# A two-layer hybrid trunk on one core: both attentions in blocks of two heads, and the turns of the experts' inner rows moved

## The reference

```
z = modulate(rms_norm(x)) @ w_in             # one projection feeds four mixers
A: p = softmax(q1 k1 / sqrt 32) - lam * softmax(q2 k2 / sqrt 32)
   ya = rms_norm(p @ v) * (1 - lam_init)     # 4 heads, 64 value columns a head
B: yb = hyena(z)                             # long convolution
C: window attention with sinks, 4 heads of 64, norm and rotation on q and k
D: yd = conformer convolution
acc = sum over the four of sigmoid(z @ w_gate + b) * (y @ w_branch)
x = x + g1 * (acc @ w_out)
experts: top 2 of 16; u = silu(x @ w1[e]) * (x @ w3[e]); y = u @ w2[e]
x = x + g2 * (weighted sum of the two experts' rows)
```

## Time and profile before

| | |
|---|---|
| median of the runs | 1540.88 us |
| profiled execution, its own time | 1544.08 us |
| its span | 1542.1 us |
| TensorE busy | 1445.8 us, 94% |
| VectorE, ScalarE, GpSimd busy | 757.9, 277.6, 165.9 us |
| TensorE, experts of both layers, waits for ScalarE's copy L1958 | 10.0 us in 14 |
| TensorE, experts of layer 1, waits for VectorE's L2731 | 7.2 us in 8 |
| HBM rate in the slices of layer 1's experts | 379, 418, 412, 422, 420, 238 GB/s |

### The profile page before, as it was taken

How to read it: one execution, slowest core, us unless ns; L and a number is a source line. 1 busy time by engine, 2 the same in 40 slices (tenths; PEclk the granted TensorE clock), 3 DMA queues, 4 the chain that set the end, 5 groups by cost and what they waited for, 6 DMA issues and landing times. The chain is left out here.

```text
span 1542.1 us, 17006 instructions
## 1 busy us (share of the span) xinstructions
PE 1445.8 (94%) x6200; PEld 718.8 (47%) x6200; DVE 757.9 (49%) x1689; ACT 277.6 (18%) x570; POOL 165.9 (11%) x156
## 2 busy tenths in 40 slices
PE   6999999789999999999999999899989999999987
PEld 2544644344444444632323233765777875433332
DVE  4297866646555879532122223686676635211112
ACT  3201101422232210411011011110242203000000
POOL 0000011001011210021111101001001210111000
PEclk9999999989999999999999999999999999999999
DMA  9420234101223453689999986425333695999996
GB/s 380 186 98 27 74 145 164 55 28 55 82 82 141 164 191 109 275 322 420 423 425 422 418 360 237 162 85 225 127 110 137 220 374 211 379 418 412 422 420 238
DMA packets 49536, 355.55 MB, mean 231 GB/s; under 512 B 6288, under 2 KB 6672, under 8 KB 22704
## 3 DMA queue, kind: packets, MB, share of 16 engines
q1 hardware_dynamic: 41360, 330.79, 54.3%
q0 software_dynamic: 4800, 14.24, 2.5%
q10 hardware_dynamic: 3296, 9.44, 1.6%
HBM read 343.88 MB, written 10.56 MB: 230 GB/s over the span
## 5 line engine op out<-in xcount | busy, mean ns | idle before, releaser
L1209 PE MATMUL ps<-hT,ring 128*128 128x512 f32 (+1 forms) x1344 | 452.6, 492 | 1.9 <-DVE hT L2334 1.3
L1209 PEld LDWEIGHTS ps<-hT,ring 128*128 128x128 f32 x1344 | 253.8, 192 | 177.0 <-issue 157.9
L1515 PE MATMUL ps<-ring,m 128*64 128x512 f32 x624 | 277.1, 595 | 12.7 <-ACT m L1958 8.0
L1515 PEld LDWEIGHTS ps<-ring,m 128*64 128x64 f32 x624 | 81.9, 137 | 185.4 <-issue 172.7
L2296 DVE SCALAR_TENSOR_TENSOR spare<-ring,crow 128x1024 bf16<-128x1024 f32 x120 | 155.8, 1298 | 4.1
L1222 PE MATMUL ps<-ring,hT 128*128 128x512 f32 (+1 forms) x352 | 125.1, 515 | 0.0
L2021 POOL TENSOR_TENSOR wide<-wide,gates 128x512 f32<-128x512 f32 (+1 forms) x48 | 69.6, 1450 | 395.9 <-DVE gates L2473 395.9
L1517 PE MATMUL ps<-n_,m 128*64 128x512 f32 x224 | 100.0, 595 | 0.0
L1310 PE MATMUL ps<-yT,ring 128*128 128x512 f32 (+1 forms) x256 | 94.5, 492 | 2.3 <-ACT n_ L1857 2.3
L1517 PE MATMUL ps<-wide,m 128*64 128x512 f32 x208 | 93.7, 597 | 0.0
L1222 PEld LDWEIGHTS ps<-ring,hT 128*128 128x128 f32 x352 | 66.7, 190 | 55.1 <-issue 51.4
(11 more groups left out here) (389 smaller groups left out, 1699.3 us busy)
## 6 DMA issues: line engine op xcount, KB each, us to landing
ring<-w SPq DMA_DIRECT2D x39, 2048.0 KB, 11.1
ring<-win SPq DMA_DIRECT2D x52, 1024.0 KB, 4.9
ring<-wmod SPq DMA_DIRECT2D x48, 1024.0 KB, 5.0
n_<-w SPq DMA_DIRECT2D x13, 2048.0 KB
hT<-w SPq DMA_DIRECT2D x13, 2048.0 KB, 16.6
wide<-w SPq DMA_DIRECT2D x13, 2048.0 KB
ring<-wbr SPq DMA_DIRECT2D x8, 1024.0 KB, 4.8
ring<-wout SPq DMA_DIRECT2D x4, 2048.0 KB, 11.9
```

Of the source, the lines that this page charges most:

```text
L1209: last = pe.matmul(b[:, 0:W], w[:, k, jj * P:(jj + 1) * P], hT[:, k, 0:W], start=(k == 0), stop=(k == KD - 1))
L1515: pe.matmul(ps[0:HALF, bnk, :], left[:, k, 0:HALF], even[k], start=(k == 0), stop=(k == n_k - 1), skip_group_check=True)
```

## The change

The lists of both attentions are written anew. `attention` now takes the products as pairs of a gate and a branch product and gives each block of two units its share of them (`share`): scores of both units; the value steps of a tile that ended in the block before; maxima and exponentials of both, then probabilities of both; the first group of the share (a gate product); in A the means of the ended tile; the next one or two groups; the transposes of both units; the rest of the share; the ended tile's `yR`; the block's share of the passes. In layer 0's A there are nine pairs of products for eight blocks, in layer 1's nine for four; in C eight for eight and for four. The last gate product of B, in C the first of C's own branch, stands ahead of the last tile's values; C's transposes come between A's last values and their means. `settled` goes.

In the experts, `turn_u` stands in the middle of the side's up products in layer 0. In layer 1 the mixing of pair e - 1 moves behind the up products of pair e, with `turn_u` between its two tiles; pair 0 turns as before. ScalarE's, VectorE's and SyncE's programs of the experts are unchanged.

```diff
--- before.py
+++ after.py
@@ -196,22 +196,6 @@
     return [s for g in spread(main, side) for s in g]
 
 
-def settled(groups):
...
-
 def mod_steps(l, chunks):
     out = []
     for c in chunks:
@@ -380,41 +364,54 @@
             return groups + turns
         return groups[:2] + [g for t in range(TILES - 2) for g in (groups[t + 2], turns[t])] + turns[-2:]
 
-    def attention(b):
+    def share(items, parts, n):
+
+        return items[-(-n * len(items) // parts):-(-(n + 1) * len(items) // parts)]
+
+    def attention(b, products, passes, behind):
+
         units = [(t, h) for t in range(tt) for h in HEADS_OF[b]]
-        groups, turn = [], []
-        for i in range(len(units) + 2):
-            group = []
-            if i < len(units) and i % 2 == 0:
-                group += [("T", ("s" + b, l, t, h, n)) for t, h in units[i:i + 2] for n in range(2 if b == "A" else 1)]
-            if i < len(units):
-                group += [("V", ("mx" + b, l, *units[i])), ("S", ("ex" + b, l, *units[i]))]
-            if 1 <= i <= len(units):
-                group += [("V", ("p" + b, l, *units[i - 1]))]
-            groups += [group] if group else []
-            if i >= 2:
-                t, h = units[i - 2]
-                groups += [g for g in turn[:1] if g]
-                turn = turn[1:]
-                groups += [[("T", ("pT" + b, l, t, h)), ("S", ("pTout" + b, l, t, h))]]
-                if h == 3 and b == "C":
-                    groups += [[("T", ("yC", l, t)), ("S", ("yToutC", l, t))]]
-                elif h == 3:
-                    groups += [[("T", ("yA", l, t)), ("S", ("ysqA", l, t))]]
-                    turn = [[("T", ("yM", l, t)), ("V", ("yrA", l, t))], [], [("T", ("yR", l, t)), ("V", ("ynA", l, t))]]
-        return groups + [g for g in turn if g]
+        values = lambda t: [("T", ("y" + b, l, t)), ("S", ("ysqA" if b == "A" else "yToutC", l, t))]
+        out, ended = [], []
+        pairs = [units[i:i + 2] for i in range(0, len(units), 2)]
+        for n, two in enumerate(pairs):
+            out += [("T", ("s" + b, l, t, h, q)) for t, h in two for q in range(2 if b == "A" else 1)]
+            normed = ended if b == "A" else []
+            out += [s for t in ended for s in values(t)]
+            for unit in two:
+                out += [("V", ("mx" + b, l, *unit)), ("S", ("ex" + b, l, *unit))]
+            out += [("V", ("p" + b, l, *unit)) for unit in two]
+            mine = share(products, len(pairs), n)
+            ahead = 3 if b == "A" and l else 2
+            steps = [g for pair in mine for g in pair]
+            out += steps[0]
+            out += [s for t in normed for s in (("T", ("yM", l, t)), ("V", ("yrA", l, t)))]
+            out += [s for g in steps[1:ahead] for s in g]
+            for t, h in two:
+                out += [("T", ("pT" + b, l, t, h)), ("S", ("pTout" + b, l, t, h))]
+            out += [s for g in steps[ahead:] for s in g]
+            out += [s for t in normed for s in (("T", ("yR", l, t)), ("V", ("ynA", l, t)))]
+            out += [s for g in share(passes, len(pairs), n) for s in g]
+            t, h = two[1]
+            ended = [t] if h == 3 else []
+        out += behind[0] + values(tt - 1)
+        if b == "A":
+            out += turns + [("T", ("yM", l, tt - 1)), ("V", ("yrA", l, tt - 1))]
+            out += behind[1] + [("T", ("yR", l, tt - 1)), ("V", ("ynA", l, tt - 1))]
+        return out
 
     o += merge(conformer[:12], spread(prepared("A") + projections, turned(with_conformer)))
-    units = attention("A")
-    half = len(units) // 2
-    turns = [g for g in prepared("C") if g[0][0] == "T"]
+    turns = [s for g in prepared("C") if g[0][0] == "T" for s in g]
     ropes = [[("V", ("rsC", l))]] + [g for g in prepared("C") if g[0][0] == "V"]
-    o += settled(spread(conformer[12:] + gate_groups(1, False),
-                        units[:half] + spread(units[half:], ropes) + turns))
-    o += settled(spread(spread(gate_groups(0, False), turned(in_c)), attention("C")))
+    two_of = lambda groups: [groups[i:i + 2] for i in range(0, len(groups), 2)]
+    products = two_of(conformer[12:] + gate_groups(1, False))
+    early_passes = [[]] * (len(ropes) - 2) if l == 0 else []
+    o += attention("A", products[:-1], early_passes + ropes, products[-1])
+    last_gates = gate_groups(2, False)
+    o += attention("C", two_of(gate_groups(0, False)), turned(in_c), last_gates[:1])
     net, spectrum = filter_groups(l + 1) if l + 1 < DEPTH else ([], [])
 
-    last_gates = gate_groups(2, False)
+    last_gates = last_gates[1:]
     n = len(last_gates) if l == 0 else len(last_gates) // 2
     o += merge(spread(last_gates[:n], turned(behind)) + last_gates[n:], net)
     o += gate_steps(l, (4, 5))
@@ -1518,9 +1515,9 @@
                                              start=(k == 0), stop=(k == n_k - 1), skip_group_check=True)
                         return last
 
-                    def four_quarters(bnk, left, quarters):
-
-                        for k in range(4):
+                    def four_quarters(bnk, left, quarters, ks=range(4)):
+
+                        for k in ks:
                             for g, (weights, k0, rows_, cols_) in enumerate(quarters):
                                 last = pe.matmul(ps[SIDE * g:SIDE * (g + 1), bnk, :], left[:, k0 + k, rows_:rows_ + SIDE],
                                                  weights[:, k0 + k, cols_], start=(k == 0), stop=(k == 3),
@@ -1531,8 +1528,8 @@
                         whole = slice(0, FE)
                         return [(even, 0, 0, whole), (odd, 0, SIDE, whole), (even, 4, 0, whole), (odd, 4, SIDE, whole)]
 
-                    def mix_block(first, last_, signal=True):
-                        for t in range(live(l)):
+                    def mix_block(first, last_, signal=True, tiles=range(live(l))):
+                        for t in tiles:
                             for half in range(2):
                                 last = pe.matmul(ps[:, 4 + 2 * t + half, :], mixing[:, t, :],
                                                  ysb[:, half * 512:(half + 1) * 512], start=first, stop=last_,
@@ -1541,14 +1538,17 @@
                                     last.then_inc(half_mixed, 1)
                         return last
 
-                    def mix(e):
+                    def mix(e, turn=None):
 
                         if not e:
                             pe.wait_ge(pieces_ready, l + 1)
                         pe.wait_ge(mixing_ready, e + 1)
                         pe.wait_ge(y_low, base + e + 1)
                         pe.wait_ge(y_high, base + e + 1)
-                        mix_block(e == 0, e == PAIRS - 1).then_inc(y_mixed, 1)
+                        mix_block(e == 0, e == PAIRS - 1, True, range(0, 1))
+                        if turn is not None:
+                            turn_u(turn)
+                        mix_block(e == 0, e == PAIRS - 1, True, range(1, 2)).then_inc(y_mixed, 1)
 
                     def gate_and_up(e):
 
@@ -1568,8 +1568,6 @@
                             if behind_first(l, e):
                                 pe.wait_ge(side_y_ready, e)
                             four_quarters(7, side_xT, split_k(wg, wg2)).then_inc(side_gate_done, 1)
-                        if not side and e:
-                            mix(e - 1)
                         weights_landed("w3", e)
                         if not side:
                             pe.wait_ge(y_high, base + e)
@@ -1577,7 +1575,9 @@
                         if side:
                             if behind_first(l, e):
                                 pe.wait_ge(y_high, base + e)
-                            four_quarters(6, side_xT, split_k(wu, wu2)).then_inc(side_up_done, 1)
+                            four_quarters(6, side_xT, split_k(wu, wu2), range(0, 2))
+                            turn_u(e)
+                            four_quarters(6, side_xT, split_k(wu, wu2), range(2, 4)).then_inc(side_up_done, 1)
 
                     def turn_u(e):
                         pe.wait_ge(u_ready, base + e + 1)
@@ -1614,7 +1614,10 @@
 
                     def pair(e):
                         gate_and_up(e)
-                        turn_u(e)
+                        if not side and e:
+                            mix(e - 1, e)
+                        elif not side:
+                            turn_u(e)
                         if side and not e:
                             pe.wait_ge(pieces_ready, l + 1)
                         down(e)
```

More of the change, by code:

```diff
@@ L196, in merge @@
     return [s for g in spread(main, side) for s in g]
-def settled(groups):
-    groups, i = list(groups), 1
-    while i < len(groups):
-        kinds = [g[0][1][0] for g in groups]
-        if kinds[i] in ("yA", "yC") and kinds[i - 1] in ("pTA", "pTC"):
-            j = i + 1
-            while j < len(groups) and kinds[j] not in ("gate", "br", "pTA", "pTC", "yM"):
-                j += 1
-            if j < len(groups) and kinds[j] in ("gate", "br"):
```

(4 more changed lines are left out.)

## The result

The changed kernel takes 1536.63 us (median of 10 runs, 1529.62 to 1539.06). The kernel before, run beside it, took 1544.46 (1540.47 to 1547.6), more than its first three runs had shown. The ratio is 0.9944, interval 0.9926 to 0.9961: 0.56% faster, which is 8.6 us; the two medians, like the two traces, lie 7.8 us apart. Predicted were 18.7 us and the range 1513 to 1531, so less than half of the gain arrived. The later start isn't the reason: the same ratio on the 1540.88 us that the prediction started from would give 1532.3, outside the range too. The profiled executions took 1544.08 and 1536.32, spans 1542.1 and 1534.3.

The account below looks back on a forecast made before the run. TensorE was taken to be busy nearly throughout, so savings count only where it idles, runs slowly or waits. Terms -20.7 - 5.8 - 0.9 + 3.6 + 4.4 + 0.7 = -18.7 us gave 1522.2 us, range 1513 to 1531.

Parts of the forecast that it names:

- Layer 0's attentions: Attentions A and C of layer 0: most TensorE idle time goes and A's clock returns; 20.7 and 5.8 us gained.
- rival (b): Layer 0's attention A: the clock doesn't come back, as narrow products stand in one piece; 1528 us, chance 0.12.
- Ahead of w_out: Layer 0, the stretch behind attention C: no change, 0 us in the sum.
- Attentions of layer 1: Attentions A and C of layer 1: transposes wait for VectorE; A 0.9 us gained, C 3.6 us lost.
- Turns in layer 0: Layer 0's experts, eight pairs: ScalarE's copy order unchanged, idle before the down product grows 0.75 to 1.3; 4.4 us lost.
- Turns in layer 1: Layer 1's experts: waits for VectorE and ScalarE go, but weight transfers are the wall; 0.7 us lost.
- Rival (c): Layer 0's attentions: VectorE lags there too, half of the idle 15.7 and 6.6 stays; 1532 us, chance 0.07.
- (a): Experts: ScalarE's two copies overlap, last weights come earliest; -6.0 and -3.0 us instead of +5.1; 1508 us, chance 0.08.
- (d): Attention C, both layers: late modulation chunks hold up VectorE's next chain of maxima; slower, 1553 us, chance 0.05.

Follow-up runs that it names:

- experiment 2: The changed kernel with four chunks put by hand on other ring places, w_out's first no longer behind the last gate product's chunk: 1532.43 us, ratio 0.9919.
- experiment 4: The changed kernel with layer 1's old attention order: 1531.51 us; instead with experiment 3's order, experiment 2's places, layer 1's passes straight behind the probabilities: 1508.14 us.
- experiment 3: The changed kernel with ScalarE copying the turned rows before the side's up products: 1523.86 us; the same with layer 0's turn at its old place: 1530.42 us.
- experiment 5: The changed kernel without two of four mixing products in seven pairs of layer 1: 1535.83 us; the best kernel with the mixing's and turn's move undone: 1508.41 us.
- the best kernel: The changed kernel with experiment 3's ScalarE order, experiment 2's places and layer 1's passes straight behind the probabilities: 1508.14 us, run again 1509.71 us.
- experiment 1: The changed kernel with both edits of the experts undone, so only the attentions' new order remains: 1526.69 us, ratio 0.9888.

## Why the prediction was wrong

**Layer 0's attentions: right in kind, and near in size by luck.** 25.8 of 26.5 us. Two errors in it cancel: idle left is 5.1, not 1.6 (waits of 0.77, 0.39, 0.89, 1.15 and 0.55 in A, 0.40, 0.19 and 0.64 in C), and the clock gave back 8.7 us of busy time, not 5.8, as other products than the three gates had been slow too (scores of 1.56 and 1.24 us, at 339.93 and 320.41, where the same take 0.71 at 362.83). All gate products now take 7.0 to 7.1, so rival (b) falls. The rule of the Trainium skill weighed there (TensorE: Matmul & The Clock Gate, HAM oscillation) would have left 1.7 us behind at the fall after short waits only; this trace has no fall there, though short waits remain (0.77 us ahead of the transposes at 270.26, then a gate product of 7.03).

**Ahead of w_out: a term that was missing, 4.8 us.** This is the step that failed: the sum gave the stretch behind attention C nothing, without a look at where its transfers go. The prediction followed SyncE's queue past one wait only ("it now comes a gate product later in layer 1") and took for granted that the chunks of the ring keep their places. The planner's places follow the list, and the list changed. What stands in the place of that nothing is a wait of 3.12 us for 0.43, the 2.7 us that experiment 2 gives back in every trace with TensorE's, VectorE's, ScalarE's and GpSimd's orders unchanged, and 2.1 us of clock behind it, which vary. At 4.8 us in this pair of traces it is the largest single miss; its certain part alone, 2.7, is under the next one, the 3.4 of layer 1's attentions.

**Attentions of layer 1: right in kind, mis-sized.** 6.1 lost for 2.7. Idle to w_out grew from 9.5 to 13.3 us, 3.9; the sum had 2.7. In C each late pair also waits 0.48 at its second transposes, which the sum left out: 6.8 for 5.5. A is 5.8 for 5.9. The other 2.2 are TensorE's own time, above all a branch product of 1.92 and scores of 1.86 us at the lower clock straight after waits of 1.28 and 1.08. I had called the lag a price of the block form in layer 1, "the reverse of layer 0"; experiment 4 shows that most of it was where the passes stood. The same blocks with the passes placed better take 3.7 us less than the order of before (148.6 against 152.3).

**Turns in layer 0: right, mis-sized.** The reason (ScalarE's order is unchanged) is what experiment 3 shows. The stage lost 5.8 us for 4.4: a pair grew by 0.72, not 0.55, the idle by 0.58.

**Turns in layer 1: the wall is right, the loss doesn't reach the stage.** The weights are the wall, as experiment 5 shows. From the last gate product (1496.13, after 1.65 for its weights) to the last down product (1516.99) are 20.9 us, against 19.9 in the earlier trace rows: 0.9 lost for 0.7. It is the mixing's place that does this: the two traces of experiments with the mixing at its old place have 19.9, four others with it moved 20.9. But the stage as a whole doesn't lose it: with the mixing moved it takes 228.0 us (changed kernel) and 228.1 (the best kernel again), with the mixing at its old place 228.1 (experiment 1) and 228.5 (experiment 5). That it is 1.3 longer than before is thus not the mixing's doing. The 1.3 are TensorE's busy time at a clock of 0.98 for 1.00 (202.7 to 204.1), its idle time being the same; why the stage doesn't hide them stays open. The 436 GB/s of the Trainium skill that was weighed here (DMA: Bandwidth & Descriptors, section Where 436 GB/s comes from) is the ceiling of the ports; for transfers from HBM the same section has a lower one of some 358 GB/s. The slices of this stage, 412 to 422 GB/s, are above that, so it doesn't hold here.

**Range.** It had bounds for each stretch that the change edits and none for the ones behind them, where 5.9 of the 10.9 missing microseconds are (2.7, 2.1, 1.1; the last two are clock alone). Rival (c), VectorE's lag, holds in layer 1 and not in layer 0, where I had put it. Rivals (a) and (d) didn't happen: the two copies of ScalarE don't overlap, and no chain waits for a modulation chunk.

## What to carry to other kernels

When places of buffers are planned from an order, reordering changes the plan: compare who frees each transfer's place before and after, also where no step moved. Put an engine's filler straight behind the chain that it has just finished, not behind an instruction that itself waits for another engine. A result made earlier is worth nothing until the queue of the engine that takes it on is reordered as well: of two edits one alone lost 5.7 us and the other alone did nothing, and together they gained 5.4.

## What the hardware showed that I had not expected

The clock's falls don't follow from the order of instructions alone. The wait ahead of w_out is 3.12 us in the changed kernel and 3.07 in the kernel of experiment 1, with the same instructions around it; the first product then takes 9.96 us in the one and this in the other:

```profile
542.77 7.11 PE L1390 MATMUL ps<-ring,wide 128*128 128x512 f32 x16 [3.07 <-DMA ring<-wout]
```

Behind that wait the fall is the rule, not the exception: six traces have it, of 3.0 to 3.2 us, and the product takes 8.6 to 10.0 us in five of them and 7.11 in this one. In the seven traces with experiment 2's places the wait is 0.43 and the product takes 7.11 in each.

With the old order of layer 1 the gate product behind scores that waited 1.22 us takes 3.72 us before and 5.41 in the kernel of experiment 4. The stretch from w_out to the experts of layer 1, whose instructions are the same in all the kernels here, takes between 54.5 and 57.3 us, with TensorE's granted clock between 1.00 and 0.94. The changed kernel's own ten runs lie 9 us apart. So a few us between two traces say nothing of an edit unless they are found as idle time, or in a stretch at the same clock.
